# Strassen products added straight from PSUM, an earlier second weight slab, and half-tile output rows in a hybrid decoder block

## The reference

```python
xn = rms_norm(h, g_pre_mix)                       # then w_in -> q, k, v, u
mix = concat[rms_norm(window_attention(q, k, v)), rms_norm(glu(gelu(s5_ssm(u))))] @ w_o
h = h + rms_norm(mix, g_post_mix)
ff = swiglu(rms_norm(h, g_pre_ffn), w_gate, w_up, w_down)
h = h + rms_norm(ff, g_post_ffn)

def swiglu(xn, w_gate, w_up, w_down):
    hid = silu(xn @ w_gate) * (xn @ w_up)         # 2048 -> 5632
    return hid @ w_down                           # 5632 -> 2048
```

## Time and profile before

| | |
|---|---|
| median of the runs | 2688.15 us |
| profiled execution | 2688.73 us, of which the span of the slowest core (core 7) is 2687.2 us |
| spans of the eight cores | 2661.2 to 2687.2 us |
| PE busy | 2462.6 us, 92% |
| DVE busy | 1596.6 us, 59% |
| POOL busy | 1174.8 us, 44% |
| ACT busy | 763.7 us, 28% |
| granted TensorE clock, mean over the core's span | 0.964 to 0.969 |

### The profile page before, as it was taken

The page is one execution under the profiler, slowest core; times in us unless marked ns, Lnnn a source line. Parts: engine busy times, 40 slices in busy tenths (PEclk is TensorE's granted clock), DMA queues, the critical chain, the costliest instruction groups (busy, mean ns, idle before and its releaser), DMA issues.

```text
span 2687.2 us, 33771 instructions; the slowest of 8 cores (2661.2 to 2687.2 us)
## 1 busy us (share of the span) xinstructions
PE 2462.6 (92%) x12896; PEld 1204.5 (45%) x12896; DVE 1596.6 (59%) x2001; ACT 763.7 (28%) x1498; POOL 1174.8 (44%) x1048
## 2 busy tenths in 40 slices
PE   3789999777888889999999999998999999999998
PEld 1445668533443434444444444443444444444443
DVE  6636774456776768988888400017888888820003
ACT  5644443254665522121111000012212111100002
POOL 4124778523344336666666311104656666531012
PEclk9899999887999999999999999998999999999999
DMA  8474457935778787767666966649988776785557
GB/s 212 124 114 91 80 96 101 134 66 134 179 182 188 191 164 119 102 81 93 88 87 84 191 108 105 108 71 198 155 162 149 113 93 80 90 125 76 79 103 233
DMA packets 485724, 332.38 MB, mean 124 GB/s; under 512 B 181952, under 2 KB 448576, under 8 KB 477760
## 3 DMA queue, kind: packets, MB, share of 16 engines
q0 software_dynamic: 258448, 159.46, 45.8%
q1 hardware_dynamic: 227120, 170.77, 23.9%
HBM read 397.21 MB, written 54.53 MB: 168 GB/s over the span
## 4 chain that ended last, share of the span: by engine, by line
PE 70%; DVE 13%; DMA 6%; issue 5%; ACT 3%; POOL 2%; SPq 0%; POOLq 0%; DVEq 0%; ACTq 0%
PE ps L430 70%; DVE wsm.143_185 L430 1%; DVE wsm.144_186 L430 1%; DMA PT.117_159<-Pb.114_156 1%; DMA raw.140_182<-w_gate 1%; DVE M1.2_44 L430 1%; DVE xr.129_171 L430 1%; DMA raw.138_180<-w_up 1%; DVE xs.36_78 L430 1%; DVE hn.133_175 L430 1%; DMA PT.117_159<-Pb.115_157 0%; DMA uscr<-ust.74_116 0%; DVE ast.25_67 L430 0%; DVE xs.37_79 L430 0%; DVE hf.225_267 L430 0%
## 5 line engine op out<-in xcount | busy, mean ns | idle before, releaser
L430 DVE TENSOR_TENSOR hf.225_267<-ps,gpo.180_222 128x512 f32<-128x512 f32 x16 | 11.1, 691 | 243.3 <-ACT junk.135_177 L430 233.7
L430 DVE TENSOR_TENSOR wsm.144_186<-raw.140_182 128x1024 bf16<-128x1024 bf16 x88 | 104.9, 1229 | 54.1 <-DMA raw.140_182<-w_gate 53.1
L430 PE MATMUL ps<-hnT.134_176,wsm.144_186 128*128 128x512 bf16 x528 | 124.3, 386 | 11.9 <-DVE wsm.144_186 L430 8.2
L430 PE MATMUL ps<-hnT.134_176,wsm.142_184 128*128 128x512 bf16 x528 | 122.8, 383 | 2.5 <-DVE wsm.142_184 L430 2.5
L430 PE MATMUL ps<-hnT.134_176,wsm.141_183 128*128 128x512 bf16 x528 | 121.1, 379 | 0.0
L430 PE MATMUL ps<-hnT.134_176,wsm.143_185 128*128 128x512 bf16 x528 | 121.1, 379 | 0.0
L430 ACT ACTIVATE junk.135_177<-ps 128x512 bf16<-128x512 f32 x48 | 28.6, 596 | 306.5 <-PE ps L430 300.0
L430 DVE TENSOR_TENSOR wsm.141_183<-raw.137_179 128x1024 bf16<-128x1024 bf16 x88 | 110.4, 1294 | 0.6 <-DMA raw.137_179<-w_gate 0.6
L430 ACT ACTIVATE ps<-ps 128x512 f32<-128x512 f32 x32 | 18.6, 582 | 288.4 <-DVE ev.166_208 L430 140.2
L430 DVE TENSOR_TENSOR wsm.143_185<-raw.139_181 128x1024 bf16<-128x1024 bf16 x88 | 95.5, 1128 | 4.5 <-DMA raw.139_181<-w_up 4.5
L430 PE MATMUL ps<-wh.8_50,xnT.1_43 128*128 128x256 bf16 x768 | 90.4, 278 | 4.4 <-ACT v1.5_47 L430 4.4
(11 more groups left out here) (1360 smaller groups left out, 6442.2 us busy)
## 6 DMA issues: line engine op xcount, KB each, us to landing
raw.137_179<-w_gate POOLq DMA_DIRECT2D x22, 1024.0 KB, 10.3
raw.138_180<-w_up POOLq DMA_DIRECT2D x22, 1024.0 KB, 10.4
raw.140_182<-w_gate POOLq DMA_DIRECT2D x22, 1024.0 KB, 10.1
raw.139_181<-w_up POOLq DMA_DIRECT2D x22, 1024.0 KB, 10.2
xr.129_171<-x SPq DMA_DIRECT2D x16, 1024.0 KB, 6.2
hscr<-xr.129_171 SPq DMA_DIRECT2D x16, 1024.0 KB, 4.8
hf.225_267<-ffscr SPq DMA_DIRECT2D x8, 1024.0 KB, 7.9
hf.225_267<-hscr SPq DMA_DIRECT2D x8, 1024.0 KB, 11.4
```

What stands on the lines that cost most here:

```text
L430: inst = getattr(eng, m)(*a, **kw)
```

## The change

1. In `unit`, POOL does no arithmetic any more. DVE makes all five `wsm` sums. Each product is taken from PSUM into every quarter that needs it: 12 uses in all. The first use of a quarter is an ACT copy with scale +1 or -1 (four a unit), every later one a DVE addition or subtraction (eight a unit). The products are made in another order, with a special order for the first unit of block 0. `unit` returns the quarters in another order, and `gate_up` multiplies them in that order.
2. For block 0 the second slab buffer moves from 8 KB to 186 KB, `n2` from 186 KB to 0 KB and `n3` from 0 KB to 8 KB. `xcomb` makes `n1` and the sum in `b21` first.
3. `epi0` works on half tiles (128 x 1024), sixteen of them, one for every one and a half units from unit 3 to unit 25, with four buffers in place of two. Both its loads wait for the landing of slab `u - 2`. `1/rms` of all eight tiles is made once, in `rs_first`, after `down(0)`.

```diff
-        raw = [[... for o_ in oo] for oo in ((96 * KB, 8 * KB), (96 * KB, 176 * KB))]
+        raw = [[... for o_ in oo] for oo in ((96 * KB, 186 * KB), (96 * KB, 176 * KB))]
-        xe = [[... for o_ in oo] for oo in ((178, 186, 0), (0, 8, 16))]
+        xe = [[... for o_ in oo] for oo in ((178, 0, 8), (0, 8, 16))]
...
+            half(n1, b21, b11, ALU.subtract)
+            half(b21, b21, b22, ALU.add)
             half(n2, b11, b12, ALU.add)
             half(b12, b12, b22, ALU.subtract)
-            half(n1, b21, b11, ALU.subtract)
-            half(b21, b21, b22, ALU.add)
             half(n3, b11, b22, ALU.add)
...
-            G.tensor_tensor(out=m[:, 4, :, :], in0=a12, in1=a22, op=ALU.subtract)
+            V.tensor_tensor(out=m[:, 4, :, :], in0=a12, in1=a22, op=ALU.subtract)
...
+            acc = {k: [next_ev(blk), False] for k in (21, 12, 11, 22)}
+            def into(k, prod, sign):
+                o_, seen = acc[k]
+                if seen:
+                    V.tensor_tensor(out=o_, in0=o_, in1=prod, op=ALU.add if sign > 0 else ALU.subtract)
+                else:
+                    A.activation(out=o_, in_=prod, func=AF.Copy, scale=float(sign))
+                    acc[k][1] = True
+            how = {1: (lambda c: m[:, 0, c, :], n3, ((11, 1), (22, 1))),
+                   2: (lambda c: m[:, 2, c, :], b11, ((21, 1), (22, -1))),
+                   3: (lambda c: r[:, c, 0:128], b12, ((12, 1), (22, 1))),
+                   4: (lambda c: r[:, 8 + c, 128:256], n1, ((21, 1), (11, 1))),
+                   5: (lambda c: m[:, 3, c, :], b22, ((12, 1), (11, -1))),
+                   6: (lambda c: m[:, 1, c, :], n2, ((22, 1),)),
+                   7: (lambda c: m[:, 4, c, :], b21, ((11, 1),))}
+            for i in (4, 2, 5, 7, 6, 3, 1) if blk == 0 and u == 0 else (4, 3, 1, 2, 5, 6, 7):
+                lhs, rhs, uses = how[i]
+                prod = product(lhs, rhs)
+                for k, sign in uses:
+                    into(k, prod, sign)
+            return [acc[k][0] for k in (21, 12, 22, 11)]
...
-                if blk == 1 and s % 3 != 0 and s < 12:
-                    epi0(2 * (s // 3) + s % 3 - 1, 2 * s)
+                if blk == 1:
+                    for h in range(16):
+                        if (3 + 3 * h // 2) // 2 == s:
+                            epi0(h, 3 + 3 * h // 2)
...
+        def rs_first():
+            V.tensor_reduce(out=ms8[:, :], in_=fss[:, 0:8, :], axis=AX.X, op=ALU.add)
+            rstd(rs8[:, :], ms8[:, :])
+        def epi0(h, u):
+            t, k, j = h // 2, h % 4, h % 2
+            fb, hb2 = hf[:, 2 * k:2 * k + 2, 512:1024], hf[:, 8 + 2 * k:10 + 2 * k, 512:1024]
+            rows = slice(t * 128, (t + 1) * 128)
+            cs = slice(1024 * j, 1024 * j + 1024)
+            P.dma(fb, ffscr[rows, cs]..., rk=[("f", t, db) for db in (2 * j, 2 * j + 1)] + [("gu", 1, u - 2)])
+            P.dma(hb2, hscr[rows, cs]..., rk=[("h", t), ("gu", 1, u - 2)])
+            V.scalar_tensor_tensor(out=fb, in0=fb, scalar=rs8[:, t:t + 1], in1=hb2, op0=ALU.mult, op1=ALU.add)
+            P.dma(out[rows, cs]..., fb)
```

More of the change, by code:

```diff
@@ L1064, in build_nc @@
         HT = 32 * KB
-        raw = [[sb("raw", o_, [128, 16, 256], BF16) for o_ in oo] for oo in ((96 * KB, 8 * KB), (96 * KB, 176 * KB))]
+        raw = [[sb("raw", o_, [128, 16, 256], BF16) for o_ in oo] for oo in ((96 * KB, 186 * KB), (96 * KB, 176 * KB))]
         wsm = [[sb("wsm", o_, [128, 5, 8, 128], BF16) for o_ in oo] for oo in ((104 * KB, 16 * KB), (104 * KB, 184 * KB))]
-        xe = [[sb("xe", o_ * KB, [128, 8, 512], BF16) for o_ in oo] for oo in ((178, 186, 0), (0, 8, 16))]
+        xe = [[sb("xe", o_ * KB, [128, 8, 512], BF16) for o_ in oo] for oo in ((178, 0, 8), (0, 8, 16))]
         wdn = [sb("wdn", o_ * KB, [128, 4, 512], BF16) for o_ in (176, 180, 184, 188, 96, 100, 104, 108)]
@@ L1137, in unit @@
             V.tensor_tensor(out=m[:, 3, :, :], in0=a11, in1=a12, op=ALU.add)
-            G.tensor_tensor(out=m[:, 4, :, :], in0=a12, in1=a22, op=ALU.subtract)
+            V.tensor_tensor(out=m[:, 4, :, :], in0=a12, in1=a22, op=ALU.subtract)
             n1, n2, n3 = xe[blk]
             (b11, b12), (b21, b22) = XB
-            c21, c12, c11, c22 = [next_ev(blk) for _ in range(4)]
-            A.activation(out=c21, in_=product(lambda c: r[:, 8 + c, 128:256], n1), func=AF.Copy)
-            A.activation(out=c12, in_=product(lambda c: r[:, c, 0:128], b12), func=AF.Copy)
@@ L1144, in unit @@
[L1144 to L1149, removed]
@@ L1150, in unit @@
-            V.tensor_tensor(out=c22, in0=c22, in1=product(lambda c: m[:, 1, c, :], n2), op=ALU.add)
-            V.tensor_tensor(out=c11, in0=c11, in1=product(lambda c: m[:, 4, c, :], b21), op=ALU.add)
-            return c21, c12, c11, c22
+            acc = {k: [next_ev(blk), False] for k in (21, 12, 11, 22)}
[6 more added lines that the diff above has]
+                    acc[k][1] = True
@@ L1154, in gate_up @@
+            for i in (4, 2, 5, 7, 6, 3, 1) if blk == 0 and u == 0 else (4, 3, 1, 2, 5, 6, 7):
[4 more added lines that the diff above has]
+            return [acc[k][0] for k in (21, 12, 22, 11)]
         def gate_up(blk):
             for s in range(22):
-                if blk == 1 and s % 3 != 0 and s < 12:
-                    sv_ = P.prio
-                    P.prio = sv_ + 100.0
-                    epi0(2 * (s // 3) + s % 3 - 1, 2 * s)
-                    P.prio = sv_
+                if blk == 1:
+                    for h in range(16):
+                        if (3 + 3 * h // 2) // 2 == s:
+                            sv_ = P.prio
+                            P.prio = sv_ + 100.0
+                            epi0(h, 3 + 3 * h // 2)
+                            P.prio = sv_
@@ L1166, in gate_up @@
                 up = unit(blk, 2 * s + 1, wu_v, s)
-                for k, (f, t) in enumerate(((1, 0), (0, 1), (0, 0), (1, 1))):
+                for k, (f, t) in enumerate(((1, 0), (0, 1), (1, 1), (0, 0))):
                     V.tensor_tensor(out=hid[2 * s + f][:, 512 * t:512 * t + 512], in0=sg[k], in1=up[k], op=ALU.mult)
@@ L1211, in rs_of @@
             return r
-        def epi0(t, u):
-            k = t % 2
-            fb, hb2 = hf[:, 4 * k:4 * k + 4, 512:1024], hf[:, 8 + 4 * k:12 + 4 * k, 512:1024]
-            rows = slice(t * 128, (t + 1) * 128)
[L1217 to L1221, removed]
+        ms8 = sb("ms8", c1 + 2880, [128, 8], F32)
+        rs8 = sb("rs8", c1 + 2912, [128, 8], F32)
+        def rs_first():
[4 more added lines that the diff above has]
+            fb, hb2 = hf[:, 2 * k:2 * k + 2, 512:1024], hf[:, 8 + 2 * k:10 + 2 * k, 512:1024]
+            rows = slice(t * 128, (t + 1) * 128)
+            cs = slice(1024 * j, 1024 * j + 1024)
+            P.dma(fb, ffscr[rows, cs].rearrange("p (a n) -> p a n", a=2),
+                  rk=[("f", t, db) for db in (2 * j, 2 * j + 1)] + [("gu", 1, u - 2)])
+            P.dma(hb2, hscr[rows, cs].rearrange("p (a n) -> p a n", a=2), rk=[("h", t), ("gu", 1, u - 2)])
+            V.scalar_tensor_tensor(out=fb, in0=fb, scalar=rs8[:, t:t + 1], in1=hb2, op0=ALU.mult, op1=ALU.add)
+            P.dma(out[rows, cs].rearrange("p (a n) -> p a n", a=2), fb)
         def epi1(t):
@@ L1297, in build_nc @@
         down(0)
+        rs_first()
         P.prio = 900.0
```

## The result

The changed kernel takes 2655.47 us in the median, against 2688.15 us; the ratio is 0.989 with a 95% interval of 0.9855 to 0.9925. That is 20 to 39 us less, and not a difference of two per cent. The forecast of 2646 us was 9.5 us too low, inside its range.

A forecast was written before the change was run, and what follows sets the result against it. PE was taken as the bound, busy 92% of the span, so only its gaps and lower clock could be won back. 28.9 + 13.3 + 1.5 - 1.0 = 42.7 us off 2688.7 gave 2646 us, range 2630 to 2669.

The forecast's parts named there:

- B: First half of `gate_up(1)`: 34.4 us lost to PE waits and lower clock after them; the change gains 28.9 us.
- The slab wait in B: PE's 7.7 us wait for the third slab of `gate_up(1)`; POOL issuing that load earlier was to leave about 1 us.
- DVE becomes the bound: Rival in `gate_up`: DVE's stalls stay, 14.0 us of DVE a unit, time near 2840; 4% including its second road.
- Its second road: Slab loads land later than 20.7 us because DVE holds up POOL's descriptor writing; within the slower rival's joint 4%.
- The DMA engines hold B: Rival: while `epi0` runs in `gate_up(1)`, transfers need 278 us against 272 of PE work; time say 2655; 20%.
- A: Start of `gate_up(0)`: 14.8 us lost to waits and lower clock; loading the second slab earlier gains 13.3 us.
- close to a tie: After `oproj`: some 11 us of DVE work against 10.4 us of PE products; 1.5 us left as loss.
- the start of block 0 only moves its wait: Rival at the start of `gate_up(0)`: PE waits for `n3` or `wsm` instead; gain 5 not 13.3, time 2654; 15%.
- `oproj`'s gap: PE's 2.8 us gap on `Ab` late in `oproj`; half, 1.5 us, won, less 1 us for a slab load alongside.

The follow-up runs named there:

- the second profile: The changed kernel itself run and profiled once more, with no edit against it: ratio 0.9895 (0.9873 to 0.9918) to the kernel before, `gate_up(1)` 536.7 us.

## Why the prediction was right, and where it was not

*B.* Right, by its mechanism. Predicted 28.9 us on core 7, measured 31.3; in the mean of the cores 25.9 (24.7 by the second profile), as `gate_up(1)` had been less slow on the others (561.4 us in the mean, 565.9 on core 7). `gate_up(1)` in "about 537 us" is 534.59. `wsm` near 0.68 is 0.685. The load on DVE was put too high, 10.2 us a unit (85% of the stretch); it is 368.06 us in 475 / 12.08 = 39.3 units, 9.4 a unit, since 593 instructions cover 0.62 us each: instructions that follow each other without a wait start 0.60 us apart, though each is shown with 0.68. The slab wait in B went mostly by part 3's loads and not by POOL's queue.

*DVE becomes the bound* did not happen: DVE is busy 77% of the steady stretch. Its second road, slab loads held up by DVE, did not show either: POOL issues the second slab in 1.22 us, the third and those of `gate_up(1)` in 1.14.

*The DMA engines hold B* is refuted. The share did reach the top, 1.00 and 1.07 in the two stretches shown, and PE was busy 89.16 and 89.77 of 90 us in them. The estimate of 278 us of transfers in 272 us of PE work was near; the step from "saturated" to "PE waits" was not.

*A* is the step that failed: the term of 13.3 us. From the end of `oproj` 5.6 us came on core 7, and `oproj` lost as much; in the mean of the cores F gave 3.9 us with one profile of the changed kernel and 1.5 with the other. The second slab did what I said: issued at 933.53 (I wrote near 938), landed by 947.16, when DVE takes it up. What I had not followed is the third slab. I counted what the moved tiles cost DVE ("close to a tie", 1.5 us) and did not ask when the first slab's buffer comes free: product 3 needs `b12`, `b12` is overwritten only after `n2`, and `n2` now lies under `Wo`. The prediction's rival "the start of block 0 only moves its wait" (A gains 5, 2654 us) is what came true, by a wait it did not list. It had 15%, and the forecast without it 46%. That the median lies within the stated range is owed to B, and to a range wide enough to hold this rival; the median is 9.5 us from the forecast and 1.5 us from the rival's 2654. That the two profiled executions come closer to the forecast (37.8 of 42.7 us) is luck: 5.8 of these are scatter ahead of `oproj`.

*`oproj`'s gap.* I gave it +1.5 us, as POOL's `anb` no longer holds `n2` up, and −1.0 for the slab's load beside `oproj`. It went the other way, from 2.7 to 4.9 us, and `oproj` takes 353.9 in place of 352.6 us in the mean though one product fewer runs in it (three, not four): I moved a load past SP's transposes and priced POOL's queue and not SP's.

For A and `oproj` together 13.3 and 0.5 us were forecast, and 1.5 to 3.9 came in the mean: 9.9 to 12.3 us short, which is as much as the 9.5 us between forecast and median. B is 3.0 to 4.2 us short in the mean as well; the rest of the sum is within scatter.

**Open.** What part 2 is worth. Without it the ratio is 0.9917, with it 0.989 and 0.9895, and the intervals overlap. What bounds F from below was not found: each wait that I removed gave way to another.

## What to carry to other kernels

Work on an engine that is far from its bound can still be the cause, when its reads lengthen another engine's operations: look for one shape with a median at its least and a tail several times longer, and see what runs beside the long ones. Where a load is moved earlier, follow the next load of the same ring and every queue the moved one now runs beside, before counting its wait as won. A wait at the start of a stage is worth its length only if what follows has its own inputs in time.

## What the runs showed of the hardware

The DMA transpose of an `hn` tile, issued from SP, is held up by a slab load that POOL has issued some microseconds before: 1.6 us without, 4.9 to 6.6 us with it on core 7, and the delay followed the slab when the slab was moved. That POOL's writes leave DVE's two-input operations alone (684 ns beside 50.5 us of writes in 97) and its reads don't (1000 ns beside 56.6 us) I had not known before. And a DMA share of 1.07 was no sign of waiting: PE was busy 89.77 of 90 us in it.
